# An opening on x laid out by features, and LayerNorm moments taken half by half, in a stack of mixers at 256 tokens

## The reference

```python
def layer_norm(x, g, b):
    xf = x.astype(jnp.float32)
    mu = xf.mean(-1, keepdims=True)
    var = jnp.square(xf - mu).mean(-1, keepdims=True)
    return ((xf - mu) * lax.rsqrt(var + LN_EPS)).astype(x.dtype) * g + b

def swiglu(x, w_in, w_out):
    gate, up = jnp.split(x @ w_in, 2, axis=-1)
    return (jax.nn.silu(gate) * up) @ w_out

h = x
for i in range(DEPTH):                     # 2
    h = layer_norm(DN_ALPHA * h + 0.5 * swiglu(h, ffn_w_in[i, 0], ffn_w_out[i, 0]), ln_g[i, 0], ln_b[i, 0])
    ...                                    # the mixer: m
    h = layer_norm(DN_ALPHA * h + m, ln_g[i, 1], ln_b[i, 1])
    h = layer_norm(DN_ALPHA * h + 0.5 * swiglu(h, ffn_w_in[i, 1], ffn_w_out[i, 1]), ln_g[i, 2], ln_b[i, 2])
```

## Time and profile before

| | us |
|---|---|
| median of three runs | 1522.62 |
| the profiled execution | 1522.67 |
| its span | 1520.9 |
| TensorE busy, products | 1512.6 (99%) |
| VectorE busy | 968.4 (64%) |
| ScalarE busy | 755.7 (50%) |
| GpSimd busy | 131.2 (9%) |
| tile loads, issue to landing, median | 4.8 |

### The profile page before, as it was taken

How to read it: one execution, slowest core, us unless ns; L and a number is a source line. 1 busy time by engine, 2 the same in 40 slices (tenths; PEclk the granted TensorE clock), 3 DMA queues, 4 the chain that set the end, 5 groups by cost and what they waited for, 6 DMA issues and landing times.

```text
span 1520.9 us, 20479 instructions
## 1 busy us (share of the span) xinstructions
PE 1512.6 (99%) x8164; PEld 1300.4 (86%) x8164; DVE 968.4 (64%) x981; ACT 755.7 (50%) x724; POOL 131.2 (9%) x141
## 2 busy tenths in 40 slices
PE   9999999999999999999999999999999999999998
PEld 8888889888888888888888888888898888888886
DVE  5556576765567556577667655557686556785555
ACT  5454465554545454454434445455536566354442
POOL 1000020100002000024021200002002200020000
PEclk9999999999999999999999999999999999999999
DMA  8554564355545654555544455556443444455551
GB/s 311 196 192 172 213 221 166 133 218 205 192 169 188 226 191 175 211 213 203 175 163 166 171 225 186 183 203 224 168 166 141 160 144 167 166 213 202 189 187 67
DMA packets 42264, 283.71 MB, mean 187 GB/s; under 512 B 5088, under 2 KB 5536, under 8 KB 9552
## 3 DMA queue, kind: packets, MB, share of 16 engines
q1 hardware_dynamic: 38016, 270.55, 48.6%
q0 software_dynamic: 2368, 8.59, 1.7%
q10 hardware_dynamic: 1808, 3.55, 0.6%
HBM read 281.55 MB, written 1.05 MB: 186 GB/s over the span
## 4 chain that ended last, share of the span: by engine, by line
PE 99%; DMA 0%; ACT 0%; DVE 0%; SPq 0%; DVEq 0%; POOLq 0%; issue 0%; POOL 0%; ACTq 0%
PE psum L1687 21%; PE psum L1582 17%; PE psum L1585 16%; PE psum L1586 16%; PE psum L1691 11%; PE psum L1714 5%; PE psum L1721 3%; PE psum L1627 2%; PE psum L1614 2%; PE psum L1620 2%; PE psum L1594 1%; PE psum L2113 0%; DMA weights_raw<-in_weights 0%; PE psum L2076 0%; PE psum L2134 0%; PE psum L1967 0%
## 5 line engine op out<-in xcount | busy, mean ns | idle before, releaser
L914 DVE TENSOR_TENSOR weights_lo<-weights_raw,weights_hi 128x2048 fp32r<-128x2048 f32 x247 | 569.8, 2318 | 318.5 <-ACT weights_hi L434 317.2
L434 ACT ACTIVATE weights_hi<-weights_raw 128x2048 fp32r<-128x2048 f32 (+1 forms) x254 | 479.5, 1890 | 297.5 <-PE psum L1586 140.7
L1687 PE MATMUL psum<-operand,weights_hi 128*128 128x512 f32 x1376 | 327.6, 390 | 0.0
L1687 PEld LDWEIGHTS psum<-operand,weights_hi 128*128 128x128 f32 x1376 | 255.3, 188 | 51.1
L1582 PE MATMUL psum<-weights_hi,hidden_hi 128*128 128x512 f32 x480 | 187.7, 391 | 0.0
L1585 PE MATMUL psum<-weights_lo,hidden_hi 128*128 128x512 f32 x480 | 187.6, 391 | 0.0
L1586 PE MATMUL psum<-weights_hi,hidden_lo 128*128 128x512 f32 x480 | 186.8, 389 | 0.0
L1691 PEld LDWEIGHTS psum<-operand,weights_lo 128*128 128x128 f32 x1376 | 176.4, 191 | 6.7
L1691 PE MATMUL psum<-operand,weights_lo 128*128 128x256 f32 x1376 | 178.5, 283 | 0.0
L1582 PE MATMUL psum<-weights_hi,operand 128*128 128x512 f32 x384 | 151.6, 395 | 0.0
L1585 PE MATMUL psum<-weights_lo,operand 128*128 128x512 f32 x384 | 149.8, 390 | 0.0
(11 more groups left out here) (297 smaller groups left out, 1828.8 us busy)
## 6 DMA issues: line engine op xcount, KB each, us to landing
weights_raw<-in_weights SPq DMA_DIRECT2D x254, 1024.0 KB, 4.8
ln_rows<-in_ln_rows POOLq DMA_DIRECT2D x16, 512.0 KB, 6.8
weights_raw<-in_weights SPq DMA_DIRECT2D x4, 512.0 KB, 6.6
normalised<-in_x SPq DMA_DIRECT2D x2, 512.0 KB, 6.1
ret_constants<-in_ret_constants ACTq DMA_DIRECT2D x1, 1024.0 KB, 7.3
out<-normalised SPq DMA_DIRECT2D x4, 256.0 KB, 2.0
gla_w_low<-in_gla_w_low ACTq DMA_DIRECT2D x1, 512.0 KB, 5.5
att_w_small<-in_att_w_small ACTq DMA_DIRECT2D x1, 512.0 KB, 5.7
```

Source lines behind the costliest of these rows:

```text
L434: nc.scalar.activation(w_hi[:, s, whole], raw[:, s, whole], ACT.Copy).then_inc(hi_split, 1)
L914: nc.vector.tensor_tensor(w_lo[:, s, :], raw[:, s, :], w_hi[:, s, :].bitcast(F32), ALU.subtract).then_inc(lo_split, 1)
L1687: mm(banks[b // 2][:, b % 2, :], w_hi[:, slot, cols], x_both[:, c, :, :].rearrange("p a t -> p (a t)"), start=c == 0, stop=False, skip_gro ...
```

## The change

Two parts. In the opening, x comes a second time in DRAM, laid out by features (`x_turned`, 4 pieces of two chunks, 256 KB each), and is loaded into slot 2 of `raw`. Its high and low parts are made from there, so that x isn't turned. Tile 0 is laid out in DRAM by quarters and loaded in four transfers. The opening unit does both token blocks at once. Tile 2 is loaded when x's last low part is made, and x by tokens (for the residual) behind it. In LayerNorm, the mean of the first half alone is the centre of both squares; each half is squared when it is evacuated, with two sums. The variance is then the mean of the squares about that centre, less the square of the gap between the two means: VectorE adds the gap and the surplus, and POOL subtracts the surplus from the second sum in the step that adds epsilon.

```diff
-        variance = sb("variance", [P, TB])
+        moment = sb("moment", [P, TB, 4])
...
         def _(sp):
-            sp.dma_start(xn[:, 0, :], io["x"][0]).then_inc(x_loaded[0], 16)
-            for n in range(2):
-                for j in range(2):
-                    cols = slice(j * D, (j + 1) * D)
-                    sp.dma_start(raw[:, n, cols], io["weights"][n][:, cols]).then_inc(weight_loaded[n] if j else half_loaded[n], 16)
-            sp.dma_start(xn[:, 1, :], io["x"][1]).then_inc(x_loaded[1], 16)
+            first_tile = io["weights"][0].rearrange("p n -> (p n)").rearrange("(k p n) -> k p n", k=4, p=P)
+
+            def load_chunks(g):
+                sp.dma_start(raw[:, 2, g * NCOL:(g + 1) * NCOL], io["x_turned"][g]).then_inc(chunks_loaded[g], 16)
+
+            def load_quarter(k):
+                sp.dma_start(raw[:, 0, k * NCOL:(k + 1) * NCOL], first_tile[k]).then_inc(quarter_loaded[k] if k < 3 else weight_loaded[0], 16)
+
+            load_chunks(0)
+            load_quarter(0)
+            load_quarter(1)
+            load_chunks(1)
+            load_quarter(2)
+            load_quarter(3)
+            load_chunks(2)
+            sp.dma_start(raw[:, 1, 0:D], io["weights"][1][:, 0:D]).then_inc(half_loaded, 16)
+            load_chunks(3)
+            sp.dma_start(raw[:, 1, D:], io["weights"][1][:, D:]).then_inc(weight_loaded[1], 16)
+            sp.dma_start(ident, io["constants"][:, 0, :]).then_inc(ident_loaded, 16)
+            sp.wait_ge(x_lo_done, KC // 2)
             sp.dma_start(raw[:, 2, :], io["weights"][2]).then_inc(weight_loaded[2], 16)
+            for tb in range(TB):
+                sp.dma_start(xn[:, tb, :], io["x"][tb]).then_inc(x_loaded[tb], 16)
...
             def layer_norm(ln):
                 for tb in range(TB):
-                    inverse_root(ln_rstd[:, tb:tb + 1], variance[:, tb:tb + 1], 1.0, LN_EPS, 1)
+                    pool.wait_ge(surplus_ready, 2 * (ln - 1) + tb + 1)
+                    inverse_root(ln_rstd[:, tb:tb + 1], moment[:, tb, 1:2], moment[:, tb, 3:4], LN_EPS, 1, ALU.subtract)
...
             pool.wait_ge(x_loaded[1], 16)
-            pool.wait_ge(operand_ready, KC // 2)
...
                     act.wait_ge(mean_ready, 2 * (ln - 1) + tb + 1)
-                    link(nc.scalar.activation(squares[:, :], xn[:, tb, :], ACT.Square, bias=scaled_mean[:, tb:tb + 1],
-                                              scale=D ** -0.5, accum_out=variance[:, tb:tb + 1]))
-                    act.sem_inc(var_ready, 1)
+                    for b in range(2):
+                        cols = slice(b * NCOL, (b + 1) * NCOL)
+                        act.wait_ge(evacuated, 4 * (ln - 1) + 2 * tb + b + 1)
+                        link(nc.scalar.activation(squares[:, cols], xn[:, tb, cols], ACT.Square, bias=scaled_mean[:, tb:tb + 1],
+                                                  scale=D ** -0.5, accum_out=moment[:, tb, b:b + 1]))
+                        act.sem_inc(var_ready if b else first_moment, 1)
...
-            act.dma_start(ident, io["constants"][:, 0, :]).then_inc(ident_loaded, 16)
-            rows_hi("x", 0, block_acc(0), (0,))
-            quarters_hi(0)
-            rows_hi("x", 0, block_acc(0), (1,))
-            quarters_hi(1)
-            rows_hi("x", 1, block_acc(1))
+            for n in range(2):
+                x_hi_first(2 * n)
+                quarter_hi_first(n, 0)
+                quarter_hi_first(n, 1)
+                x_hi_first(2 * n + 1)
+                quarter_hi_first(n, 2)
+                quarter_hi_first(n, 3)
             split_hi(2)
             ffn(N_FFN0, 0)
...
-                        evacuated = nc.vector.scalar_tensor_tensor(
+                        nc.vector.scalar_tensor_tensor(
                             out=xn[:, tb, cols], in0=acc[:, 2 * tb + b, :], scalar=scale, in1=resid[:, tb, cols],
-                            op0=ALU.mult, op1=ALU.add, accum_out=row_sum[:, 2 * tb + b:2 * tb + b + 1])
+                            op0=ALU.mult, op1=ALU.add, accum_out=row_sum[:, 2 * tb + b:2 * tb + b + 1]).then_inc(evacuated, 1)
+                        if b == 0:
+                            dve.wait_ge(evacuated, 4 * (ln - 1) + 2 * tb + 1)
+                            nc.vector.tensor_scalar(scaled_mean[:, tb:tb + 1], row_sum[:, 2 * tb:2 * tb + 1], -2 * D ** -1.5, None,
+                                                    ALU.mult).then_inc(mean_ready, 1)
                         if held and (tb, b) == (1, 0):
                             rows_lo("ln2", 0, block_acc(0), (0,))
-                    link(evacuated)
+                    dve.wait_ge(evacuated, 4 * (ln - 1) + 2 * tb + 2)
                     sums = [row_sum[:, 2 * tb + b:2 * tb + b + 1] for b in range(2)]
-                    nc.vector.tensor_scalar(scaled_mean[:, tb:tb + 1], sums[0], sums[1], -D ** -1.5,
-                                            ALU.add, ALU.mult).then_inc(mean_ready, 1)
+                    gap = moment[:, tb, 2:3]
+                    nc.vector.tensor_scalar(gap, sums[1], sums[0], 1.0 / D, ALU.subtract, ALU.mult)
                     link(nc.vector.tensor_scalar(minus_mean[:, tb:tb + 1], sums[0], sums[1], -1.0 / D, ALU.add, ALU.mult))
+                    dve.wait_ge(first_moment, 2 * (ln - 1) + tb + 1)
+                    nc.vector.scalar_tensor_tensor(out=moment[:, tb, 3:4], in0=gap, scalar=gap, in1=moment[:, tb, 0:1],
+                                                   op0=ALU.mult, op1=ALU.subtract).then_inc(surplus_ready, 1)
...
-            rows_lo("x", 0, block_acc(0), (0,))
-            quarters_lo(0)
-            rows_lo("x", 0, block_acc(0), (1,))
-            quarters_lo(1)
-            rows_lo("x", 1, block_acc(1))
+            for n in range(2):
+                x_lo_first(2 * n)
+                quarter_lo_first(n, 0)
+                quarter_lo_first(n, 1)
+                x_lo_first(2 * n + 1)
+                quarter_lo_first(n, 2)
+                quarter_lo_first(n, 3)
             split_lo(2)
...
+                def products(n, k, x, w, start=False, stop=False):
+                    for tb in range(TB):
+                        last = mm(out[:, tb, :], x[:, 4 * n + k, tb * P:(tb + 1) * P], w[:, n, k * NCOL:(k + 1) * NCOL],
+                                  start=start, stop=stop, skip_group_check=True)
+                    return last
...
                 for n in range(2):
                     for k in range(4):
                         hi_by_hi(n, k)
+                        lo_by_hi(n, k)
                         if k:
-                            lo_by_hi(n, k - 1)
-                        if k > 1:
-                            hi_by_lo(n, k - 2)
...
+                            hi_by_lo(n, k - 1)
+                    hi_by_lo(n, 3).then_inc(weights_used, 1)
 
             pe.wait_ge(warm_ready, 1)
-            warm(8)
+            warm(10)
+            opening_unit(pairs[0])
             pe.wait_ge(ident_loaded, 16)
-            turn_x1 = turn_rows("x", xn, 1, block_acc(1), x_loaded[1], lambda b: 16)
-            opening_unit(pairs[0], turn_rows("x", xn, 0, block_acc(0), x_loaded[0], lambda b: 16), turn_x1)
-            first_unit(N_FFN0, pairs[0], "x", turn_x1, blocks=(1,))
             ffn(N_FFN0, 0)
```

More of the change, by code:

```diff
@@ L102, in build @@
         work = bank[:, 4:8, :]
+        x_raw = raw[:, 2, :].rearrange("p (c t) -> p c t", c=KC)
         as_pair = lambda t: t.rearrange("p (a b) t -> p a (b t)", a=2)
@@ L201, in build @@
         warm_ready = sem("warm_ready")
-        half_loaded = [sem(f"half_loaded{n}") for n in range(2)]
+        chunks_loaded = [sem(f"chunks_loaded{g}") for g in range(KC // 2)]
+        quarter_loaded, half_loaded = [sem(f"quarter_loaded{k}") for k in range(3)], sem("half_loaded")
+        x_hi_done, x_lo_done = sem("x_hi_done"), sem("x_lo_done")
         first_hi, first_lo = sem("first_hi"), sem("first_lo")
@@ L258, in build @@
         order = ["ln1", "gla", "ln2", "ln3", "ln4", "ret", "ln5", "ln6", "mrg", "ln7"]
-        turns, at = {"x": 0}, KC // 2
+        turns, at = {}, 0
         for what in order:
@@ L1600, in turn_normed, with first_unit @@
                 return turn_rows(f"ln{ln}", xn, tb, block_acc(tb), xn_ready, lambda b: 4 * (ln - 1) + 2 * tb + b + 1)
-            def first_unit(n, out, what, turn_second, blocks=range(TB)):
-                for tb in blocks:
+            def first_unit(n, out, what, turn_second):
+                for tb in range(TB):
                     t = slice(tb * P, (tb + 1) * P)
@@ L1838, in warm, with opening_unit @@
                     mm(work[:, 3, 0:P], squares[:, 0:P], squares[:, 0:P], start=True, stop=True)
-            def opening_unit(out, turn_first, turn_second):
-                def by_hi(n, k, operand, start):
-                    mm(out[:, 0, :], operand[:, 4 * n + k, 0:P], w_hi[:, n, k * NCOL:(k + 1) * NCOL], start=start, stop=False,
-                       skip_group_check=True)
+            def opening_unit(out):
```

(21 more changed lines are left out.)

41 lines of the change are left out of this document (21 added, 20 removed).

## The result

| | before | after |
|---|---|---|
| median, us (runs) | 1522.59 (15) | 1525.22 (15) |
| lowest to highest | 1522.48 to 1522.90 | 1524.37 to 1527.22 |
| the profiled execution | 1522.67 | 1525.06 |
| its span | 1520.9 | 1523.3 |
| TensorE busy | 1512.6 | 1511.1 |

The times after are 1.0019 times those before, with a 95% interval of 1.0012 to 1.0026. By the medians that is 2.6 us slower, where 1.55 was forecast. The times are also spread wider, over 2.9 us instead of 0.4. Eleven of them lie between 1524.4 and 1525.7 and four between 1526.8 and 1527.2, with nothing between these groups.

What follows compares the result with a forecast made beforehand. TensorE was taken to bound the kernel (99% of the span). Opening +1.8 us and LayerNorms -0.25 us gave +1.55 us on 1522.67, so 1524.2 us, with a range of 1520.6 to 1526.0.

Steps and rivals of the forecast that it cites:

- main forecast: Whole kernel: 1523.3 to 1525.4 us, centred on 1524.2, about 0.1% slower, chance 0.55.
- the forecast's 1.8: Opening: transposes of the first hidden block start later than 25.30; +1.8 us taken, from +1.0 to +2.2.
- a sign of being wrong: Whole kernel: wrong if L1796 starts before 25.3, the six LayerNorm waits are gone, or the granted clock dips before 30 us.
- The bound: Whole kernel: 99% of the span is TensorE, so an edit counts only through its waits or its removable work.
- Start of the products: Opening: first loads land by 5.3, products start at 5.9 at the latest and end at 16.8 or earlier.
- The added wait: Opening: tile 2, requested only after x's last low part (12.3), lands at 17.15; TensorE idles 2.3 us, starts it at 19.1.
- Rival B: Opening: TensorE's clock falls in the new idle time, tile 2's products run at 1.2 GHz until 30.4; 1527.5 us, chance 0.12.
- The six LayerNorms: LayerNorms 1 and 3 to 7: each gives 0 to 0.2 us, 0.1 taken, -0.6 us in all; from -2.9 to +0.3.
- rival A: LayerNorm: POOL's small step isn't held, the 0.48 us wait goes six times, -2.9 us; 1521.5 us, chance 0.22.
- the sum of 0.26 for two small steps: LayerNorm: VectorE's two added small operations, the gap and the surplus, take 0.26 us together.
- LayerNorm 2 and 8: LayerNorm 2: two small operations make a 0.2 us wait; LayerNorm 8, the tail: +0.15 us, from -0.25 to +0.3.
- Rival C: Opening: tile 2's load isn't late and the hidden block has no wait, -2.8 us; 1519.6 us, chance 0.08.

## Why the prediction was right, and where it was off

**The number.** The median of 1525.22 lies inside the main forecast of 1523.3 to 1525.4, by 0.2 us. The order of what is late in the opening was foreseen; that the number held is in part luck. The opening cost 1.05 us more than the forecast's 1.8, and the clock fell, which the main forecast had left out and I had named as a sign of being wrong. Tile 3's chain hid the fall in both profiles of the whole change. Six of its fifteen times, and the median of the opening alone (1526.22), lie outside the range.

**The bound** was read rightly: only TensorE's waits counted, and 1.5 us less busy time on it brought nothing.

**Start of the products.** At 5.9 at the latest was the step; it was 5.27. Their end, 16.8 at the latest, was 17.3.

**The added wait** is the mis-sized term. I had the first half of tile 1 land at 9.7 by counting units of 0.63 us back from x block 1's landing in the kernel before (11.56). It landed at 10.8, where ScalarE's copy starts after 1.5 us without data. The first piece was there by 3.5, earlier than I had allowed, so the eight units of 256 KB behind it came at 0.92 us each on average; the runs show the rate, not its reason. Every step behind it kept its length, and every time was off by about that: request of tile 2 13.40 (12.3), its copy 18.36 (17.15), tile 2 on TensorE 20.38 (19.1), tile 3's copy 23.26 (22.2), turn of the hidden block 28.15 (27.15). That is 1.0 of the 1.05 us by which the opening was short. The two copies of one MB, x by tokens between them and the order of what is late next were as forecast, and the runs that take x by tokens out of the queue, or x by features out of the slot, show both causes by themselves.

**The clock.** Rival B was given 0.12 and came true as a mechanism, not in its size. The clock fell 2.6 us after the last product, though at the program's end it had stayed at 1.00 for over 4 us: that row was no bound. Its cost wasn't 3.3 us because B let the slow products run until 30.4, all of tile 2; the clock was back at 23.3, and tile 3's chain hid most of it: TensorE waited 0.6 us for the hidden block, where it waited 2.1 us in the opening alone, without a fall until then. What it does cost shows in the spread. That the group at 1527 is the fall in the second stretch, where it is exposed, fits the profile of the opening alone (1526.84, fall at 28.7) and the smaller spread with both stretches filled, but no profile caught the whole change in that group.

**The six LayerNorms.** Forecast 0.1 us each, by POOL slipping in between centring and low part, and a wait of 0.1 to 0.3 that stays: the profile shows that, with 0.17. By the starts of the two turns the trace gave 0.12 to 0.14 each. The Trainium skill ("SBUF — State Buffer", section Who interferes with whom), on a lock between VectorE's operations with two SBUF inputs and GpSimd's, agrees with what the idle VectorE did to POOL's steps (0.30 instead of up to 0.93 us), and rival A, which had POOL free, fell. I had the hold in one direction only. VectorE's small surplus step, 0.22 us elsewhere, takes 0.48 in block 1 of these six, until POOL's piece of a low part, 2.41 us from 194.77 on, is over:

```profile
L988 DVE SCALAR_TENSOR_TENSOR moment<-moment x16: 219/220/488, 187.6 to 1517.1; 128x1 f32<-128x1 f32 x16
```

In the kernel before, the centring stood there and was held in the same way, 1.02 us against 0.74. So the sum of 0.26 for two small steps was probably too high by what that hold covers, and the 0.11 us of POOL's new form was missing in it.

**LayerNorm 2 and 8.** Forecast +0.2 and +0.15. In LayerNorm 2 the new wait is 0.28 us, for a low part by `rows_lo` (L958), a neighbour of the one that I named; the shift there grows by 0.15 to 0.2. In LayerNorm 8 it is 0.26 in all, so that term was too small. In block 0, which I had costed at nothing, POOL's first step is held for 0.91 us, and VectorE gets to block 1's evacuation 0.13 us later against the products than before. In block 1 the normalised halves come another 0.13 us later, counted from that evacuation:

```profile
1518.06 0.59 POOL L348 TENSOR_SCALAR ln_rstd<-moment 128x1 f32<-128x1 f32 x1 [4.31 <-ACTq L479]
1518.74 0.57 POOL L349 TENSOR_TENSOR ln_rstd<-ln_rstd,minus_half 128x1 f32<-128x1 f32 x1
1519.41 1.41 DVE L998 SCALAR_TENSOR_TENSOR normalised<-residual,ln_rstd,ln_rows 128x512 f32<-128x512 f32 x2 [0.92 <-POOL ln_rstd L349]
```

**Rival C**, tile 2 not late, was wrong for this change. But with its two obstacles removed the kernel comes close to C's 1519.6 (1519.87).

## What to carry to other kernels

A load that borrows a slot of a ring stops the ring: count what is queued behind the wait that guards the slot, to the second tile and to whoever stands behind that tile's copies. When TensorE has new idle time, price a fall of its clock in and just behind each idle stretch, and ask whether other work covers the slow products there; filling only the first stretch moved the fall to where it cost more. And before moving VectorE's work out of POOL's way, look at who wants that work: a wait of 0.17 us went, and one of 0.14 grew to 0.47.

## What the runs showed of the hardware that I had not expected

- The granted clock fell 2.6 us after the last product in one execution. In three others it fell only after products had started again: 0.8 us after, behind a stretch of 2.1 us (the opening alone, where a stretch of 3.0 us had passed at 1.00 before); 1.2 us after, behind 3.0 us (the whole change, second profile); and 1.1 us after, behind 2.0 us (x in its own place).
- A 1 MB load took 1.2 us longer (9.4 against 8.1 or 8.2) when TensorE ran warm-up products beside the loads, three profiles against three, while the load behind it took as long as ever (11.1 and 11.2). Not explained.
- The hold between VectorE and POOL goes both ways, and to steps on 128 numbers: 0.30 to 0.93 us on POOL, 0.22 to 0.49 us on VectorE.
